# Expert down weights asked for by ScalarE, on its own DMA queue, in a decoder step on Trainium2

## The reference

```python
hgu = xb @ w_gu[e] + b_gu[e]            # 1024 x 2048: gate and up
gate = jnp.minimum(hgu[:, :D_FF], SWIGLU_LIMIT)
up = jnp.clip(hgu[:, D_FF:], -SWIGLU_LIMIT, SWIGLU_LIMIT)
act = (up + 1.0) * gate * jax.nn.sigmoid(SWIGLU_ALPHA * gate)
return act @ w_down[e] + b_down[e]      # 1024 x 1024
```

## Time and profile before

| | |
|---|---|
| median of 3 runs | 1320.51 us (1316.22 to 1322.36) |
| the profiled execution | 1318.21 us, its span 1316.5 us |
| TensorE busy | 1254.5 us, 95% of the span |
| VectorE, ScalarE busy | 525.1 us (40%), 213.8 us (16%) |
| moved over DMA | 438.32 MB; SyncE's queue 437.89 MB, ScalarE's 0.04 MB |
| up products, L1140 | 2048 matmuls, 464.9 us |
| down products, L1151 | 1024 matmuls, 229.4 us |

### The profile page before, as it was taken

One profiled execution on the slowest core, in us unless ns is written; L12 is line 12 of the kernel. 1 busy time (PEld: TensorE's weight loads), 2 busy tenths in 40 slices (PEclk: granted clock), 3 DMA queues, 4 the chain that ended last, 5 costly groups with the idle time before them and its releaser, 6 DMA issues.

```text
span 1316.5 us, 16973 instructions
## 1 busy us (share of the span) xinstructions
PE 1254.5 (95%) x6259; PEld 544.9 (41%) x6259; DVE 525.1 (40%) x1152; ACT 213.8 (16%) x421; POOL 46.6 (4%) x106
## 2 busy tenths in 40 slices
PE   6999998889899999999999999999999999999997
PEld 4765687644333333333333333333333333333333
DVE  2683444755833333334333333333333333333323
ACT  2451111152111111111111111111111111111112
POOL 5100001100000000000000000000000000000000
PEclk9999999999999999999999999999999999999999
DMA  8331110446799999999999999999999999999951
GB/s 247 105 130 65 64 51 14 140 171 247 301 365 428 429 428 428 430 430 428 428 428 430 430 428 428 428 430 430 428 428 428 430 429 428 428 428 430 428 237 40
DMA packets 54486, 438.32 MB, mean 333 GB/s; under 512 B 10538, under 2 KB 17863, under 8 KB 29850
## 3 DMA queue, kind: packets, MB, share of 16 engines
q1 hardware_dynamic: 54336, 437.89, 80.5%
q10 hardware_dynamic: 122, 0.04, 0.0%
HBM read 432.89 MB, written 5.02 MB: 333 GB/s over the span
## 4 chain that ended last, share of the span: by engine, by line
PE 54%; DMA 37%; DVE 5%; issue 2%; ACT 1%; POOL 0%; SPq 0%; DVEq 0%; POOLq 0%; ACTq 0%
DMA ring<-in_expert_w_down 37%; PE bank L1140 13%; PE bank L1151 12%; PE bank L598 8%; PE bank L1079 3%; PE bank L1109 2%; PE bank L774 2%; PE bank L596 2%; PE bank L1248 1%; PE bank L683 1%; PE bank L695 1%; PE bank L693 1%; PE bank L1161 1%; DMA X<-in_x_sample 1%; PE bank L1087 1%
## 5 line engine op out<-in xcount | busy, mean ns | idle before, releaser
L1140 PE MATMUL bank<-ring,SC 128*64 128x512 f32 x2048 | 464.9, 598 | 12.7 <-DMA ring<-in_expert_w_gu 10.9
L1140 PEld LDWEIGHTS bank<-ring,SC 128*64 128x64 f32 x2048 | 140.3, 137 | 303.2 <-issue 268.6
L1151 PE MATMUL bank<-ring,SC 128*64 128x512 f32 x1024 | 229.4, 594 | 3.5 <-DMA ring<-in_expert_w_down 3.3
L2111 DVE TENSOR_TENSOR SC<-bank,gmoe 128x512 f32<-128x512 f32 x32 | 22.1, 692 | 447.0 <-PE bank L1087 447.0
L1151 PEld LDWEIGHTS bank<-ring,SC 128*64 128x64 f32 x1024 | 71.7, 137 | 154.7 <-issue 133.8
L2129 DVE TENSOR_TENSOR X<-X,bank 128x512 f32<-128x512 f32 x124 | 79.7, 684 | 108.3 <-PE bank L1109 103.5
L598 PE MATMUL bank<-xT,ring 128*128 128x320 f32 x384 | 114.9, 447 | 6.6 <-ACTq L1346 5.6
L1515 ACT ACTIVATE SC<-bank 128x512 f32<-128x512 f32 x32 | 19.1, 597 | 438.2 <-PE bank L1079 438.2
L1079 PE MATMUL bank<-XS,SC 128*64 128x512 f32 x384 | 87.9, 592 | 0.6 <-DVE SC L2105 0.6
L598 PEld LDWEIGHTS bank<-xT,ring 128*128 128x128 f32 x384 | 72.0, 195 | 36.6 <-ACTq L1346 7.5
L1109 PE MATMUL bank<-SC 64*128 64x512 f32 x240 | 67.7, 641 | 0.0
(11 more groups left out here) (480 smaller groups left out, 1013.0 us busy)
## 6 DMA issues: line engine op xcount, KB each, us to landing
ring<-in_expert_w_gu SPq DMA_DIRECT2D x128, 2048.0 KB, 23.0
ring<-in_expert_w_down SPq DMA_DIRECT2D x64, 2048.0 KB, 24.4
ring<-in_w_in SPq DMA_DIRECT2D x7, 2048.0 KB, 7.8
ring<-in_w_out SPq DMA_DIRECT2D x2, 2048.0 KB, 8.4
ring<-in_ple_gate_w SPq DMA_DIRECT2D x4, 1024.0 KB, 15.2
out_gdn_s<-Sf SPq DMA_DIRECT2D x1, 2048.0 KB, 9.4
X<-in_x_prompt SPq DMA_DIRECT2D x2, 512.0 KB, 6.3
SC<-in_ple_w SPq DMA_DIRECT2D x1, 1024.0 KB, 5.3
```

The source lines that it names most:

```text
L1140: last = mm(PB[j][SL * h:SL * h + SL, :], xg[:, c % 4, c // 4, :], w[:, FF * h + 512 * j:FF * h + 512 * j + 512], start=(c == 0), stop=(c ...
L1151: last = mm(PB[4][SL * h:SL * h + SL, :], hid[:, 2 * (c - NGU) + kk, :], w[:, D * kk + 512 * h:D * kk + 512 * h + 512], start=(c == NGU an ...
L2111: tell(V.tensor_tensor(xg, PB[7][:, :].rearrange("p (j h s) -> p j h s", j=4, h=2), bc(gmoe[:, :, :].rearrange("p h j -> p j h"), 3, SL), ...
```

## The change

SyncE's loop asks for up weights alone. ScalarE gets a function `load_down(b)`, called in its `expert` between the copies of the up product and the copy of the down product, for blocks 1 to 30: it reads the expert number of block b into a register and asks for the two down pairs of block b on its own queue, behind the same waits on `w_used` as before. Block 0's and block 31's down weights stay with SyncE, as do the weights of the last gate. The numbers of the waits, the slots and TensorE's work are the same.

```diff
--- before.py
+++ after.py
@@ -385,10 +385,6 @@
                 for c in range(0, NGU, 2):
                     sp.wait_ge(sem("w_used"), used(b, c + 1))
                     load_pair(sp, e, c)
-                e = sp.value_load(etab[0:1, bass.ds(b, 1)], min_val=0, max_val=NE - 1)
-                for c in range(NGU, NCK, 2):
-                    sp.wait_ge(sem("w_used"), used(b, c + 1))
-                    load_pair(sp, e, c)
             e = sp.value_load(etab[0:1, bass.ds(last_b, 1)], min_val=0, max_val=NE - 1)
             for i in range(0, NDN, 2):
                 sp.wait_ge(sem("w_used"), used(last_b, i + 1))
@@ -1531,6 +1527,12 @@
                 act.wait_ge(sem("gt"), b + 1)
                 A(sg, gt, ACT.Sigmoid, scale=ALPHA).then_inc(sem("sig"), 1)
 
+            def load_down(b):
+                e = b if type(b) is int else act.value_load(etab[0:1, bass.ds(b, 1)], min_val=0, max_val=NE - 1)
+                for c in range(NGU, NCK, 2):
+                    act.wait_ge(sem("w_used"), used(b, c + 1))
+                    load_pair(act, e, c)
+
             def expert(b, age):
                 if age >= 1:
                     gate(b - 1)
@@ -1541,6 +1543,7 @@
                 take_rows(b + 1)
                 take_hidden(b)
                 if age >= 1:
+                    load_down(b)
                     take_y(b - 1)
                     take_select(b - 1, 5)
```

## The result

The change is slower: 1332.89 us median of 6 runs (1329.93 to 1335.16), against 1321.33 of 6 runs of the kernel before on the same chip (1315.02 to 1325.60). The ratio is 1.0099, with a 95% interval of 1.0068 to 1.0129. A second series, 10 runs beside 27 of before, gave 1.0066 (1.0039 to 1.0092). The profiled execution of after has a span of 1333.3 us.

What follows compares the result with a forecast made beforehand. TensorE's work was taken to bound early expert blocks (28.15 us), weight transfers the later ones (29.37 us). Terms 0 + 0 + 7.2 + 2.6 - 0.4 gave +9.4 us: 1327.6 on the profile, 1329.9 on the median, stated 1329, range 1318 to 1341.

Steps and rivals of the forecast that it cites:

- the sum: Whole kernel: all terms added, 0 + 0 + 7.2 + 2.6 - 0.4 = +9.4 us.
- SyncE's and ScalarE's work: Per block: issues removed from SyncE and added to ScalarE cost 0 us; the down product's copy starts some 0.4 us later.
- the cover of 9 us: ScalarE's later copy to yS is hidden, since its user, the scatter, starts 9 us later; without it 12 us.
- An even share of the engines: Two full queues share the engines evenly, so 4 MiB of down pairs move at the cost of 4 MiB of up pairs.
- Lead lost: Expert blocks: the fourth up pair lands two pairs later, so the 28.15 us blocks end about six blocks earlier, +7.2 us.
- The last block: Without 2.6 us to spare at the fourth up pair, +9.8 instead of +7.2 us; a down weight wait goes, -0.4.
- the wait at D1: Last block: TensorE's wait for the second down pair goes, -0.4 us.
- A: Rival: loads are still served in the old order, every landing as before, 0 us, 1318 to 1320; chance 0.13.
- B: Rival: two queues move more where down and up pairs flow together, up to +2%, 1310; chance 0.11.
- C: Rival: two queues move less, far end -3% or +27 us, a third of it 1337 to 1339; chance 0.14.
- D: Rival: ScalarE's queue gets much less than half, down pairs come late, up to 5 us a block; chance 0.04.
- The stretch behind the last transfer: Sign at the kernel's end: the time after the last transfer grows by 9 us.

Runs made afterwards that it cites:

- e_issue_tiny: Kernel before, SyncE keeping all weights, with ScalarE also reading the expert number, waiting and issuing two 32 byte loads a block; ratio to before 1.0005.
- the two halves: The change in blocks 1 to 15 only, and in blocks 16 to 30 only; ratios to the kernel before 0.9998 and 1.0073.
- e_after_again: The changed kernel run once more, without edits; ratio to the kernel before 1.0066.
- e_second_half: The change in blocks 16 to 30 only, SyncE issuing the down pairs of blocks 1 to 15; ratio to the kernel before 1.0073.
- e_all_by_scalar: Against the change, ScalarE issues all expert weights from block 2's up weights on and the gate weights, in SyncE's former order; ratio to the kernel before 1.0018.
- e_issue_only: Kernel before, SyncE keeping all weights, with ScalarE also issuing two 4 KB loads a block into a scratch tile; ratio to before 1.0040.
- e_split_waited: Kernel before, the second up pair and second down pair each loaded as two 1 MiB loads with a wait per slot; ratio to before 1.0026.
- e_second_pair_only: Only the second down pair of each block is issued by ScalarE, the first stays with SyncE; ratio to the kernel before 1.0051.
- e_late_place: Against the change, ScalarE asks for a block's down pairs in the next block, behind its sigmoid; ratio to the kernel before 1.0315.

## Why the prediction was right

Direction and mechanism were right; 1332.9 us lies inside the range of 1318 to 1341, and against its own time the change cost 10.3 us in the stretch where the sum said 9.4. That these are so near is in part luck: the lead lost came out 1.0 us under its term and the last block 1.9 over. On the two series of runs the cost is 1.0 and 0.7%, which is 13 and 9 us.

- **SyncE's and ScalarE's work, 0 us.** Held: TensorE has no wait for ScalarE in the loop, and e_issue_tiny is 0.8 us over before. The copy to yS does start later, 0.56 us behind the end of the down product (819.10 + 7.04 = 826.14, the copy at 826.70) where it was 0.04 before (813.51 and 813.55); the sum had 0.4, and the cover of 9 us takes it in.
- **An even share of the engines.** Held. In the change each queue brings a pair in 9.8 us while both have work, and 4.9 was the time of a pair with one queue. Of the down pairs D0 lands after 13.8 us, within the 12 to 18 forecast, and D1 after 20.2, outside it; only their median of 14.7 is inside. This was the step that the rows of before could only suggest. The Trainium skill (DMA: Bandwidth & Descriptors, Queues, rings and completion order) has each engine go round-robin over its queues, packet by packet; the trace agrees with it, by these 9.8 us a pair.
- **Lead lost, 7.2 us.** The mechanism is shown by the two halves; the size was 6.2 up to block 31. The number of 28.15 us periods fell from eleven to six, five fewer, where the prediction had about six fewer. U3 came 9.1 us later than the 829.4 of before, not 9.8: TensorE starts it at 844.98, and less the 6.5 us by which the stretch starts later that is 838.5, against the 839.2 forecast. The forecast had D0 and D1 through when U3 lands. D1 is not: it lands 1.5 us after U3, and at a half share these 1.5 us are the missing 0.7 us of U3.
- **The last block, +2.2 us.** It was 4.1. The wait at U3 is there (3.56 us), and as U3 came 9.0 us later than before and TensorE only 6.2, it added 2.8 where the sum had 2.6; the wait at D1 went, as forecast. But behind the wait came what the sum lacked: the same 16 matmuls took 5.33 us and not 3.65, at a granted clock of 0.57 in that window, so partly at 1.2 GHz, after TensorE had stood still for 3.6 us. This 1.7 us is the term that was left out. It is there in the other two kernels with the same wait too (5.13 us in e_after_again, 5.22 in e_second_half).
- **Rivals.** A (the order stays) falls with the landing times and e_all_by_scalar. B and C (another rate) fall: 428 to 429 GB/s and 29.37 us in both kernels. D (ScalarE's queue starved) falls as well; TensorE has no wait for down weights.
- **The stretch behind the last transfer.** The last gate weights land at 1254.09 + 16.3 = 1270.4 before and at 1270.94 + 8.2 = 1279.1 after, which leaves 46.1 and 54.2 us to the end of the span: 8.1 us longer, where 9 were forecast.
- **The level.** 1329 was forecast and 1332.9 measured. 0.9 us of the 3.9 is the sum; the other 3 are within the scatter of the executions, in which the part ahead of the experts alone varies by up to 9.6 us over the profiles.

## What to carry to other kernels

When one queue of loads already runs at the engines' full rate, its order is a schedule: moving a part of it to another issuer's queue gives no rate, and lets the moved loads pass what is needed sooner. Count how far each load lands ahead of its use, and subtract the bytes that will now pass it; the worst of these, and the last block's above all, is the price. And a shift against a stream that binds anyway is paid once, at the end, not per block, so look at what order the last loads have.

## What the runs showed of the hardware beside this

- **A piece of a load has a price at full rate.** e_issue_only adds 256 pieces of 32 bytes a block, 16 for each of 16 engines, and the period grows by 0.16 us. e_split_waited turns 256 pieces of 16 KB into 512 of 8 KB, again 16 more for each engine, with not one byte more, and the period grows by 0.15 us. Both make about 10 ns a piece, in which whatever the end of a load costs an engine is contained; the two loads more per block are common to both. e_issue_tiny, with two pieces a block, grew it by 0.02 to 0.03 us. The windows show it as a lower rate at full share of the engines, here e_issue_only, then e_split_waited:

```profile
700.00:900.00 200.00, 193.69 (x947) 68.43 (x945) 69.58 (x161) 21.96 (x40) 0.00 (x0) 1.00 1.01 426
```

```profile
700.00:900.00 200.00, 193.33 (x947) 69.03 (x945) 69.54 (x161) 22.71 (x40) 0.00 (x0) 1.00 1.01 426
```

- **A wait can cost more than its length, and its length alone does not decide it.** Behind the waits of 0.99 us in the change the next 16 up matmuls take 3.65 us, the same as without one. Behind 3.56 us they take 5.33, at a granted clock of 0.57, and behind 6.10 us in e_second_half 5.88, at 0.50 in the first 4 us. Between these it goes both ways: behind 2.23 us in e_second_half (at 931.64) they take 5.35, at 0.62 (932 to 936 us), and behind 3.06 us in e_second_pair_only 3.65, at 1.00 (1242 to 1246 us); in e_late_place it is 3.65 behind 2.58 us (811.58) and 5.35 behind 2.27 (870.38).
